# Twelve reciprocal roots in a transformer kernel: an integer seed with three Newton steps against ScalarE's square root with one

## What is computed

```python
def rms_norm(x, g):
    xf = x.astype(jnp.float32)
    y = xf * lax.rsqrt(jnp.mean(xf * xf, axis=-1, keepdims=True) + EPS)
    return (y * g.astype(jnp.float32)).astype(x.dtype)

q = (_rms_norm(cq, mla_q_norm) @ w_q_up)         # low ranks: 256 and 128 columns
q = _rms_norm(q, mla_q_qknorm)                   # heads: 96 or 64 columns each
y = rms_norm(y.reshape(b, s, SSD_GROUPS, SSD_NORM_GROUP), ...)   # gated rows: 8 groups of 256
```

## Time and profile before

| | |
|---|---|
| median of 3 executions | 2256.97 us (2256.54 to 2258.96) |
| the profiled execution | 2257.74 us |
| its span in the trace | 2255.9 us |
| TensorE busy | 2044.9 us, 91% |
| VectorE busy | 1690.4 us, 75% |
| ScalarE busy | 1312.4 us, 58% |
| mean granted TensorE clock | 0.934 |
| read from memory | 494.25 MB, mean 220 GB/s |

### The profile page before, as it was taken

How to read it: one execution, slowest core, us unless ns; L and a number is a source line. 1 busy time by engine, 2 the same in 40 slices (tenths; PEclk the granted TensorE clock), 3 DMA queues, 4 the chain that set the end, 5 groups by cost and what they waited for, 6 DMA issues and landing times. The chain is left out here.

```text
span 2255.9 us, 27933 instructions
## 1 busy us (share of the span) xinstructions
PE 2044.9 (91%) x11029; PEld 1726.4 (77%) x11029; DVE 1690.4 (75%) x2255; ACT 1312.4 (58%) x1921; POOL 0.2 (0%) x4
## 2 busy tenths in 40 slices
PE   7877999994779999999999999969999988889989
PEld 4746778873677888878787887759987777878987
DVE  5766788756468998998999899958755755667873
ACT  2354534345347777777777777746664644445652
POOL 0000000000000000000000000000000000000000
PEclk8886999996679999999999999989999998889999
DMA  7631598832026998999899899845423442224542
GB/s 301 255 112 38 207 336 307 306 114 80 1 94 244 369 352 321 355 355 339 344 361 352 330 353 351 311 184 174 165 94 116 165 147 91 98 79 166 184 159 106
DMA packets 70089, 497.18 MB, mean 220 GB/s; under 512 B 8000, under 2 KB 8256, under 8 KB 10688
## 3 DMA queue, kind: packets, MB, share of 16 engines
q1 hardware_dynamic: 69664, 494.28, 59.6%
q10 hardware_dynamic: 288, 1.05, 0.1%
HBM read 494.25 MB, written 1.05 MB: 220 GB/s over the span
## 5 line engine op out<-in xcount | busy, mean ns | idle before, releaser
L337 DVE TENSOR_TENSOR wlo<-ring,whi 128x1024 fp32r<-128x1024 f32 (+2 forms) x845 | 1017.1, 1216 | 311.5 <-ACT whi L385 290.1
L385 ACT ACTIVATE whi<-ring 128x1024 fp32r<-128x1024 f32 (+2 forms) x845 | 885.8, 1054 | 558.3 <-PE ps L235 487.8
L235 PE MATMUL ps<-whi,hT 128*128 128x256 f32 (+2 forms) x912 | 315.3, 346 | 29.4 <-DVE hTl L291 12.6
L235 PE MATMUL ps<-wlo,hT 128*128 128x256 f32 (+2 forms) x912 | 310.3, 340 | 0.0
L235 PE MATMUL ps<-whi,hTl 128*128 128x256 f32 (+2 forms) x912 | 309.8, 340 | 0.0
L235 PE MATMUL ps<-whi,xg 128*128 128x512 f32 (+1 forms) x768 | 293.3, 382 | 5.1 <-DVE wlo L337 4.9
L235 PE MATMUL ps<-whi,xgl 128*128 128x512 f32 (+1 forms) x768 | 289.2, 377 | 0.0
L235 PE MATMUL ps<-wlo,xg 128*128 128x512 f32 (+1 forms) x768 | 289.2, 377 | 0.0
L235 PE MATMUL ps<-whi,hf 128*128 128x512 f32 x528 | 212.3, 402 | 12.5 <-DVE ffn_w L291 6.3
L235 PEld LDWEIGHTS ps<-whi,hT 128*128 128x128 f32 x912 | 178.7, 196 | 56.2 <-issue 13.5
L235 PE MATMUL ps<-wlo,hf 128*128 128x512 f32 x528 | 210.0, 398 | 0.0
(11 more groups left out here) (278 smaller groups left out, 2689.4 us busy)
## 6 DMA issues: line engine op xcount, KB each, us to landing
ring<-in_wstream SPq DMA_DIRECT2D x462, 1024.0 KB, 4.9
ring<-in_wstream SPq DMA_DIRECT2D x4, 832.0 KB, 5.4
ring<-in_wstream SPq DMA_DIRECT2D x6, 256.0 KB, 2.7
cst<-in_cst SPq DMA_DIRECT2D x1, 1028.0 KB, 9.3
x<-in_x SPq DMA_DIRECT2D x1, 1024.0 KB, 13.3
work<-in_bias ACTq DMA_DIRECT2D x2, 512.0 KB, 5.6
ring<-in_wstream SPq DMA_DIRECT2D x2, 512.0 KB, 4.8
out_x<-x SPq DMA_DIRECT2D x1, 1024.0 KB, 4.1
```

Of the source, the lines that this page charges most:

```text
L235: i = self.e.matmul(out, lhsT, rhs, start=start, stop=stop, skip_group_check=True)
L337: i = self.e.tensor_tensor(K.wlo[:, q % NS, 0:cols], src, hi.bitcast(F32), ALU.subtract)
L385: i = self.e.activation(K.whi[:, q % NS, 0:cols], K.ring[:, m % RING, at:at + cols], ACT.Copy)
```

## The change

`rstd` no longer makes a seed. ScalarE takes the square root of the mean plus EPS (`act_roots`, one activation for all values of the place, with EPS as bias from a column of constants), VectorE takes the reciprocal of it and does one Newton step in three instructions. The division by the number of columns moves into the scale of the squares, so that `ssq` holds the mean itself. At the heads ScalarE now waits for VectorE's last sum before it takes the root, and there two calls of `act_root_ahead` stand around the root, one for Sqrt and one for Exp; ahead of the last squares of the merged and the gated rows stands one for Sqrt. The masked sums of the mixing layers, which the change's title names too, are in this diff not touched.

```diff
-    def rstd(self, y, ssq, n, dim, key=None, own=True):
-        K = self.K
-        v, t, g = K.r_v[:, 0:n], K.r_t[:, 0:n], K.r_i[:, 0:n]
-        self.ts(v, ssq, 1.0 / dim, EPS, ALU.mult, ALU.add, own=own)
-        self.ts(g, v.bitcast(I32), 1, None, ALU.logical_shift_right)
-        self.ts(y.bitcast(I32), g, -1, 0x5F3759DF, ALU.mult, ALU.add)
-        for n in range(3):
-            self.stt(t, y, -0.5, v, ALU.mult, ALU.mult)
-            self.tt(t, t, y, ALU.mult)
-            self.stt(y, t, 1.5, y, ALU.add, ALU.mult, key=key if n == 2 else None)
+    def rstd(self, y, ms, n, root, key=None):
+
+        t = self.K.r_t[:, 0:n]
+        self.wait_ge(self.K.act, root)
+        self.recip(y, self.K.sd[:, 0:n])
+        self.stt(t, ms, EPS, y, ALU.add, ALU.mult)
+        self.stt(t, t, -0.5, y, ALU.mult, ALU.mult)
+        self.stt(y, t, 1.5, y, ALU.add, ALU.mult, key=key)
...
+def act_roots(K, a, n, key):
+
+    a.act(K.sd[:, 0:n], K.ssq[:, 0:n], ACT.Sqrt, bias=K.col("eps"), key=key)
...
-def act_root_ahead(K, a):
+def act_root_ahead(K, a, fn=ACT.Sqrt):
 
-    a.act(K.sd[:, 2:3], K.cst("ones")[:, 0:1], ACT.Sqrt, own=False)
+    a.act(K.ahead[:, 0:1], K.cst("ones")[:, 0:1], fn, own=False)
...
 def act_head_norms(K, a, s, vs, n, d):
...
-        a.act(sq, w, ACT.Square, key=(s, "sq", u), own=False)
+        a.act(sq, w, ACT.Square, scale=d ** -0.5, key=(s, "sq", u), own=False)
+    act_root_ahead(K, a)
+    a.wait_ge(K.dve, (s, "ss", len(vs) - 1))
+    act_roots(K, a, n * len(vs), (s, "sd"))
+    act_root_ahead(K, a, ACT.Exp)
...
-    v.rstd(K.rs[:, 0:m], K.ssq[:, 0:m], m, d, key=(s, "rs"))
+    v.rstd(K.rs[:, 0:m], K.ssq[:, 0:m], m, (s, "sd"), key=(s, "rs"))
...
-        a.act(K.sbuf2[:, 0:128], K.proj[:, i, CKV:CKV + 128], ACT.Square, accum=K.ssq[:, 2 + i:3 + i], key=(s, "lowss") if i else None)
+        a.act(K.sbuf2[:, 0:256], K.proj[:, i, CQ:CQ + 256], ACT.Square, scale=1.0 / 16, accum=K.ssq[:, i:i + 1])
+        a.act(K.sbuf2[:, 0:128], K.proj[:, i, CKV:CKV + 128], ACT.Square, scale=128 ** -0.5, accum=K.ssq[:, 2 + i:3 + i])
+    act_roots(K, a, 4, (s, "low", "sd"))
...
+    act_root_ahead(K, a)
     act_merged_squares(K, a, s, (1,))
+    act_roots(K, a, 6, (s, "merged", "sd"))
...
-    v.wait_ge(K.act, (s, "lowss"))
-    v.ts(K.ssq[:, 2:4], K.ssq[:, 2:4], 2.0, None, ALU.mult)
-    v.rstd(K.rs[:, 0:4], K.ssq[:, 0:4], 4, 256)
+    v.rstd(K.rs[:, 0:4], K.ssq[:, 0:4], 4, (s, "low", "sd"))
...
-    v.wait_ge(K.act, (s, "oss"))
-    v.rstd(K.rs[:, 0:6], K.ssq[:, 0:6], 6, 256)
+    v.rstd(K.rs[:, 0:6], K.ssq[:, 0:6], 6, (s, "merged", "sd"))
...
     a.split_to(K.parts["gs"][0] + NS - 1)
+    act_root_ahead(K, a)
     squares(1536)
+    act_roots(K, a, 16, "ysd")
...
-    v.wait_ge(K.act, "yss")
-    v.rstd(K.rs[:, 0:16], K.ssq[:, 0:16], 16, 256)
+    v.rstd(K.rs[:, 0:16], K.ssq[:, 0:16], 16, "ysd")
```

More of the change, by code:

```diff
@@ L1291, in act_mixer @@
     for i in range(2):
-        a.act(K.sbuf2[:, 0:256], K.proj[:, i, CQ:CQ + 256], ACT.Square, accum=K.ssq[:, i:i + 1])
-        a.act(K.sbuf2[:, 0:128], K.proj[:, i, CKV:CKV + 128], ACT.Square, accum=K.ssq[:, 2 + i:3 + i], key=(s, "lowss") if i else None)
+        a.act(K.sbuf2[:, 0:256], K.proj[:, i, CQ:CQ + 256], ACT.Square, scale=1.0 / 16, accum=K.ssq[:, i:i + 1])
+        a.act(K.sbuf2[:, 0:128], K.proj[:, i, CKV:CKV + 128], ACT.Square, scale=128 ** -0.5, accum=K.ssq[:, 2 + i:3 + i])
+    act_roots(K, a, 4, (s, "low", "sd"))
     act_gained(K, a, (s, "low"), K.low, 3, lambda j: K.col(f"mq{l}", j) if j < 2 else K.col(f"mkv{l}"))
@@ L1343, in act_merged_squares @@
             a.act(K.sbuf2[:, 0:c1 - c0], K.xn[:, i, c0:c1], ACT.Square, accum=K.ssq[:, 3 * i + n:3 * i + n + 1],
-                  scale=1.0 if c1 - c0 == 256 else float(np.sqrt(0.5)), key=(s, "oss") if i and n == 1 else None)
+                  scale=(c1 - c0) ** -0.5)
 def dve_mixer(K, v, l):
@@ L2305, in squares @@
             for g in (n0 // 256, n0 // 256 + 1):
-                a.act(K.sbuf2[:, 0:256], K.X[:, i, 256 * g:256 * g + 256], ACT.Square, accum=K.ssq[:, 8 * i + g:8 * i + g + 1],
-                      key="yss" if i and g == 7 else None)
+                a.act(K.sbuf2[:, 0:256], K.X[:, i, 256 * g:256 * g + 256], ACT.Square, scale=1.0 / 16, accum=K.ssq[:, 8 * i + g:8 * i + g + 1])
     for n0, n, use in row_groups(K, a, "z", KT):
@@ L2759, in memory @@
         K.r_t = sb("r_t", [128, 32])
-        K.r_i = sb("r_i", [128, 32], I32)
         K.nm3, K.den3, K.rd3, K.lse3, K.wt3 = (sb(n, [128, 3, 2, 8]) for n in ("nm3", "den3", "rd3", "lse3", "wt3"))
@@ L2772, in memory @@
         K.along = K.cbm.rearrange("p b t -> p (b t)")
-        K.sd = sb("sd", [128, 4])
+        K.sd = sb("sd", [128, 32])
+        K.ahead = sb("ahead", [128, 1])
         aux = sb("aux", [128, 2560])
@@ L2906, in pack_cols @@
     out[:, a:a + 16] = (10000.0 ** (-np.arange(0, 32, 2, dtype=np.float64) / 32)).astype(np.float32)[None]
+    out[:, COLS["eps"][0]] = EPS
     a = COLS["router"][0]
```

## The result

| | before | after |
|---|---|---|
| median | 2257.97 us (4 executions, 2256.54 to 2259.45) | 2234.57 us (4 executions, 2231.88 to 2237.21) |
| profiled execution, its span | 2257.74, 2255.9 us | 2233.72, 2231.9 us |
| TensorE busy | 2044.9 us, 11029 products | 2027.3 us, 11029 products |
| mean granted TensorE clock | 0.934 | 0.939 |
| table loads of ScalarE | 31 | 39 |

The ratio is 0.9896 (95% interval 0.9879 to 0.9913). The change makes the kernel 23.4 us faster, not 6.0; the range had ended at 2246.0.

The account below looks back on a forecast made before the run. TensorE's multiplications were taken to set the time over long stretches, with short handovers between. Terms -2.9 + 0.4 - 2.6 + 0.4 - 1.3 = -6.0 us took 2256.97 to 2251.0 us; range 2246.0 to 2256.5.

Parts of the forecast that it names:

- the second kind: Short stretches between long multiplications, where engines hand small work to each other; only there could a change of roots gain.
- low ranks: Low ranks, two layers: shorter root while TensorE stands idle behind it, 1.45 us less each, -2.9 us together.
- merged: Merged rows, two layers: shorter root while TensorE stands idle, 1.30 us less each, -2.6 us together.
- ck with mln: Heads of ck and mln: ScalarE's later squares and loads outweigh VectorE's gain, 0.2 us late per layer, +0.4 us.
- gated: Gated rows: load and root delay ScalarE's next weight copy, and TensorE waits for its split, +0.4 us.
- first window: First window: delayed copies stay covered, costing nothing; the load for Exp ahead of the first softmax goes, -1.3 us.
- The clock: TensorE's restarts behind the merged rows meet the clock's rise well (2247.0 us, chance 0.16) or badly (2255.0 us, 0.20).
- The slower side: At the three windows ScalarE's weight copies queue behind loads and root and hold TensorE back: 2262.1 us, chance 0.06.
- A switch costs twice its row: Each ScalarE table switch from or to Sqrt costs 1.28 us more than its load row: 2259.0 us, chance 0.03.
- The merged gain taken back: Later ScalarE weight copies or another wait take back the merged rows' gain: 2253.6 us, chance 0.12.
- Less than it says: The change does less than its title: TensorE's instructions stay the same, no masked sum moves; no term, no chance given.

Follow-up runs that it names:

- e1: The kernel before with only 32 unused bytes per partition added behind `cols`, no root changed: 2246.40 us, ratio 0.9960.
- e2: The kernel before with only 32 unused bytes added ahead of `aux`, so `hT` stays in place: 2238.34 us, ratio 0.9927.
- e6: The changed kernel with small tensors rearranged so `hT`, `aux`, `xg` and others keep the addresses of the kernel before: 2251.84 us, ratio 0.9985.
- e7: The changed kernel with small tensors swapped, `hT` at its address before, `aux` and `xg` at their changed addresses: 2234.11 us, ratio 0.9909.
- e5: The changed kernel timed once more, unedited, against the kernel before: 2240.54 us, ratio 0.9928.
- e11: As e6, but with the old seed and Newton steps again at heads and gated rows: 2249.46 us, ratio 0.9977.

## Why the prediction was wrong

The step that failed is one sentence of the first part: "A change of roots can only gain in the second kind", that is, outside the long stretches of products. From it followed a sum made of twelve places only. I read `cols` with one column more, `r_i` deleted and `sd` widened in the diff and gave them no line, not even a bound. By the runs they were worth 9 us, more than all roots. The range failed with it, since all its ends were made of handovers, loads and clock.

- **Placement, not in the sum.** e1 shows it by itself: 0.9960, 9 us less (5 to 13). It is two effects: the experts, the dense part and others that hold `hf`, `xg` or `yT` gain (e2, where only these move: 16 us), and products with `hT` lose, since `hT` went from distance 64 to 96 (e1 against e2: 8 us).
- **The roots, the whole of my sum, -6.0.** Single terms held: low ranks -1.45 (forecast -1.45), merged -1.26 (-1.30), ck with mln +0.1 (+0.2), gated +0.6 (+0.4), first window -1.6 (-1.3). In the time they show as 3.4 us (e6 against before on its chip, 0 to 7) and, by the ratios across two chips, as 4 (e7 against e2) and 7 (e5 against e1). So 6.0 may stand or may be nearly twice too large; the times can't tell. e11, with four of the twelve places, had 0.9977 for 0.9976.
- **The clock, a rival.** Both restarts behind the merged rows were met, one each way. Layer 0, windows before and after (PE, PEld, DVE, ACT, POOL, PEclk, DMA share, GB/s):

```profile
218.00:220.00 2.00, 0.65 (x4) 0.28 (x3) 2.00 (x4) 1.43 (x4) 0.00 (x0) 0.79 0.89 262
220.00:222.00 2.00, 2.00 (x9) 1.64 (x10) 2.00 (x6) 0.00 (x0) 0.00 (x0) 1.00 1.03 426
```

```profile
216.00:218.00 2.00, 1.07 (x3) 0.91 (x4) 2.00 (x6) 0.46 (x2) 0.00 (x0) 0.50 0.90 377
218.00:220.00 2.00, 2.00 (x6) 1.58 (x5) 1.69 (x5) 0.00 (x0) 0.00 (x0) 0.50 1.00 385
```

  Before, the products with `hT` began at 219.92 at full clock. Now they begin at 216.93, 3.0 us sooner, but at half clock until about 220: the eighth of them starts at 221.63 before and at 220.06 now, so 1.6 us are left. In layer 1 the first products had a pitch of 0.43 us before (from 632.15) and have 0.23 now (from 624.73). So the mechanism was right and the two about cancelled. Elsewhere it did not cancel: the profiled execution after has a mean clock of 0.939 for 0.934, and e5, the same kernel, needed 6 us more at a median clock of 0.935 to 0.936. Of the 23.4 us of the first measurement I put 9 to placement (e1) and 3 to 7 to the roots; 7 to 11 remain. The clock can carry about 5 of them, by an estimate: over all executions of these runs, each kernel taken by itself on its chip, 0.001 less of mean clock goes with 1.2 us more, and the profiled execution before had 0.934 (of its four timed ones no clock is known) where the four after had 0.938 or 0.939. What is left of the remainder is not explained, nor why those four all had so high a clock.
- **The slower side** (copies held back at the windows) did not come: TensorE waited for no split in the first window, though the copies started 3.4 us later behind the last squares than before (3.3 worked out).
- **A switch costs twice its row**: refuted, above. **The merged gain taken back**: refuted by TensorE's wait, 6.13.
- **"Less than it says"**: TensorE's instructions are the same, as said, but on other addresses they took another time. No rival asked whether the products themselves might take another time.

## What to carry to other kernels

An edit that adds, drops or resizes any buffer moves all that are allocated behind it, so compare the addresses of the two programs before costing anything else, and when a small edit gives an unexpected gain in a stretch it doesn't touch, count the products per 100 us there. Test it by the old kernel with a pad before crediting the algorithm: here a pad alone gave 9 to 16 us, the twelve new roots 3 to 7. Where long products with fp32r set the time, try the 256-byte residues of the held half against the moving half and choose by width, as the table shows, and measure; a theory that fits six kernels can still be wrong, and the seventh is cheap.

## What the runs showed of the hardware that I had not expected

- A 512-column product in fp32r, back to back at full clock, takes 227.6 ns when held and moving half start at the same byte modulo 256, 229.1 at 192, and 232.4 to 234.3 at the six other distances tried. With 256 columns the same distance 0 is among the worst (119.8 to 120.0, against 113.5 to 117.8 at 64). The Trainium skill (TensorE: Matmul & The Clock Gate, Step-by-step: what each phase is for) says that TensorE reads the two halves through two independent ports, so that loading the next weights takes nothing from the running product. The runs differ with that by up to 2.9%: the pitch depends on where the two lie to each other modulo 256 bytes. What lies behind it, no run shows.
- The same work at a mean clock 0.02 lower in one stretch cost 5.5 of 201 us, and whole executions of one kernel spread over 13 us (e1, 2237.36 to 2250.17) on one chip, where the four of the first measurement agreed within 5.3.
